# A depthwise convolution moved to TensorE, in 32-column tiles over four stacked shifts

## What is computed

```python
def _conformer_conv(h, w_pw1, b_pw1, w_dw, b_dw, ln_g, ln_b, w_pw2, b_pw2):
    u = h @ w_pw1 + b_pw1                                  # 1024 -> 2048
    u = u[..., :D_MODEL] * jax.nn.sigmoid(u[..., D_MODEL:])
    pad = (CONV_WIDTH - 1) // 2
    c = lax.conv_general_dilated(u, w_dw[:, None, :].astype(u.dtype),
        window_strides=(1,), padding=[(pad, pad)],
        dimension_numbers=("NWC", "WIO", "NWC"),
        feature_group_count=D_MODEL) + b_dw                # one filter of 31 taps per feature
    c = jax.nn.silu(_layernorm(c, ln_g, ln_b))
    return c @ w_pw2 + b_pw2
```

## Time and profile before

| | us |
|---|---|
| median of 3 runs | 1868.45 (1865.5 to 1893.15) |
| the profiled execution | 1865.6 |
| its span in the trace | 1863.8 |
| PE busy | 1720.8 (92%) |
| DVE busy | 1224.1 (66%) |
| ACT busy | 820.9 (44%) |
| GpSimd busy | 39.3 (2%) |
| mean granted TensorE clock | 0.966 of full speed |

### The profile page before, as it was taken

One profiled execution on the slowest core, in us unless ns is written; L12 is line 12 of the kernel. 1 busy time (PEld: TensorE's weight loads), 2 busy tenths in 40 slices (PEclk: granted clock), 3 DMA queues, 4 the chain that ended last, 5 costly groups with the idle time before them and its releaser, 6 DMA issues.

```text
span 1863.8 us, 29337 instructions
## 1 busy us (share of the span) xinstructions
PE 1720.8 (92%) x11365; PEld 1585.7 (85%) x11365; DVE 1224.1 (66%) x1756; ACT 820.9 (44%) x1229; POOL 39.3 (2%) x23
## 2 busy tenths in 40 slices
PE   7869999997888999999989879999999989689998
PEld 7857899996677999999988679998999989589997
DVE  4778575656767666766668867565666654866665
ACT  4556453335553434534352164334434344744433
POOL 0000000000013000000000000000000000000000
PEclk9979999998998999999999989999999999789999
DMA  7610245453234545445444035544445444035544
GB/s 269 213 46 1 91 181 191 180 188 116 102 103 149 188 180 192 169 176 195 173 145 134 1 125 203 193 179 176 174 170 201 169 148 168 1 104 213 190 179 159
DMA packets 53291, 285.93 MB, mean 153 GB/s; under 512 B 5872, under 2 KB 6128, under 8 KB 30704
## 3 DMA queue, kind: packets, MB, share of 16 engines
q1 hardware_dynamic: 52224, 281.46, 42.0%
q0 software_dynamic: 1008, 3.67, 0.6%
HBM read 284.05 MB, written 1.05 MB: 153 GB/s over the span
## 4 chain that ended last, share of the span: by engine, by line
PE 82%; DVE 11%; ACT 4%; issue 2%; DMA 0%; DVEq 0%; SPq 0%; ACTq 0%
PE bank L869 18%; PE bank L871 18%; PE bank L870 18%; PE bank L1052 9%; PE bank L1021 3%; PE bank L1023 3%; PE bank L1025 3%; DVE proj L1842 3%; PE bank L883 2%; PE bank L1109 1%; PE bank L1068 1%; PE bank L1089 1%; ACT whi L438 1%; DVE nmax L1559 1%; DVE att L1557 1%
## 5 line engine op out<-in xcount | busy, mean ns | idle before, releaser
L869 PE MATMUL bank<-hthi,whi 128*128 128x256 f32 x2144 | 607.9, 284 | 1.9 <-DVE wlo L1348 1.8
L870 PE MATMUL bank<-htlo,whi 128*128 128x256 f32 x2144 | 607.2, 283 | 0.0
L871 PE MATMUL bank<-hthi,wlo 128*128 128x256 f32 x2144 | 607.1, 283 | 0.0
L1342 DVE TENSOR_TENSOR wlo<-raw,whi 128x2048 fp32r<-128x2048 f32 x175 | 401.5, 2294 | 97.1 <-ACT whi L438 97.0
L869 PEld LDWEIGHTS bank<-hthi,whi 128*128 128x128 f32 x2144 | 411.6, 192 | 7.3 <-DVE wlo L1348 2.2
L870 PEld LDWEIGHTS bank<-htlo,whi 128*128 128x128 f32 x2144 | 411.6, 192 | 4.7
L871 PEld LDWEIGHTS bank<-hthi,wlo 128*128 128x128 f32 x2144 | 411.6, 192 | 0.0
L438 ACT ACTIVATE whi<-raw 128x2048 fp32r<-128x2048 f32 x175 | 334.2, 1910 | 35.5 <-PE bank L871 27.3
L521 ACT ACTIVATE tr<-tr 128x256 f32<-128x256 f32 x132 | 55.6, 421 | 656.7 <-DVE tr L1431 656.7
L1431 DVE TENSOR_TENSOR tr<-bank,rb 128x512 f32<-128x512 f32 x132 | 91.2, 691 | 231.0 <-PE bank L871 230.8
L1348 DVE TENSOR_TENSOR wlo<-raw,whi 128x1024 fp32r<-128x1024 f32 x174 | 214.6, 1233 | 23.2 <-ACT whi L446 23.0
(11 more groups left out here) (249 smaller groups left out, 2111.8 us busy)
## 6 DMA issues: line engine op xcount, KB each, us to landing
raw<-in_stream SPq DMA_DIRECT2D x176, 1024.0 KB, 5.2
raw<-in_stream SPq DMA_DIRECT2D x176, 512.0 KB, 3.5
wide<-in_wide POOLq DMA_DIRECT2D x7, 512.0 KB, 4.0
x<-in_x SPq DMA_DIRECT2D x1, 1024.0 KB, 5.5
out<-x SPq DMA_DIRECT2D x2, 512.0 KB, 2.9
wide<-in_const SPq DMA_DIRECT2D x1, 960.0 KB, 15.7
const<-in_const SPq DMA_DIRECT2D x1, 897.0 KB, 12.8
cols<-in_cols SPq DMA_DIRECT2D x1, 340.0 KB, 7.9
```

What stands on the lines that cost most here:

```text
L869: nc.tensor.matmul(out, whi_, mhi, start=start, stop=False)
L870: nc.tensor.matmul(out, whi_, mlo, start=False, stop=False)
L871: return nc.tensor.matmul(out, wlo_, mhi, start=False, stop=stop)
L1342: V.tensor_tensor(wlo[:, s, 0:UA], raw[:, s, 0:UA], whi[:, s, 0:UA].bitcast(F32), ALU.subtract)\
```

## The change

Every tap now runs on TensorE, and no diagonal is made on the chip.

- The 128 features of a chunk are four groups of 32. For each group a tile `stacked` holds four copies of its rows of `conv_u`, shifted by 0, 1, 2 and 3 tokens, on partitions 0 to 31, 32 to 63, 64 to 95 and 96 to 127. ACT starts one DMA for each copy, 16 per chunk, within SBUF (`stack`, 32 partitions x 284 elements, 36 KB each). Four chunks' tiles fit in what is free of `xn`, `att` and `proj`.
- One matmul then sums four taps of one group: 128 rows, weights 128 x 32, output on the 32 partitions of that group in the bank. Eight shifts by four groups are 32 matmuls per chunk (`convolve`), 256 in all, plain float32. `convolve(c)` is placed two chunks behind PW1; the last two stand behind it.
- The weights of the taps, 8 x 512 KB, come by DMA from a new input. GpSimd starts these eight in the second feed-forward block, one every second unit.
- ACT adds the bias of each chunk (`biased`), three chunks behind its own `stack`. The sums for the mean of chunks 0 to 4 stand ahead of `convolve(6)`, those of 5 to 7 behind `convolve(7)`. Subtraction and squaring are cut in four pieces where there were two.

```diff
+STACK = 4
+GROUP = P // STACK
+SHIFTS = -(-TAPS // STACK)
+UPITCH = 288
+SLOTS = 4
+BEHIND = 2
...
+        conv_bank = [acc[c % 4][:, (c // 4) * T:(c // 4 + 1) * T] for c in range(8)]
+        mean_bank, var_bank = tp[0][:, 0:T], tp[1][:, 0:T]
...
                 if n == 2:
-                    pool.wait_ge(s_ldi, 16)
-                    pool.wait_ge(s_ldc, 16)
                     pool.wait_ge(s_ol, 16)
                     pool.wait_ge(s_x, 12)
...
-                    for c, k, cnt, part, at in diag_runs:
-                        ins = nc.gpsimd.tensor_tensor(
-                            diag[part][:, at:at + cnt, :], ident.unsqueeze(1).to_broadcast([P, cnt, P]),
-                            dw[:, c, k:k + cnt].unsqueeze(2).to_broadcast([P, cnt, P]), ALU.mult)
...
+                    for c in range(8):
+
+                        pool.wait_ge(s_useb, U_F2 + 2 + 2 * c)
+                        pool.dma_start(tap_w[c].rearrange("p g q n -> p (g q n)"), taps_d[c]).then_inc(s_tap, 16)
...
+            def stack(c):
+
+                act.wait_ge(s_glu, c + 1)
+                if c >= SLOTS:
+                    act.wait_ge(s_dw, c - SLOTS + 1)
+                for g in range(STACK):
+                    for j in range(STACK):
+                        act.dma_start(stacked[c % SLOTS][g][j * GROUP:(j + 1) * GROUP, 0:UPITCH - STACK],
+                                      conv_u[g * GROUP:(g + 1) * GROUP, c, j:j + UPITCH - STACK])\
+                            .then_inc(s_stk[c % SLOTS], 16)
+
+            def biased(c):
+
+                act.wait_ge(s_dw, c + 1)
+                nc.scalar.activation(conv_c[:, c, :], conv_bank[c], ACT.Identity, bias=col("b_dw", c)).then_inc(s_cc, 1)
...
+                        stack(c)
+                        if c > BEHIND:
+                            biased(c - BEHIND - 1)
+            for c in range(7 - BEHIND, 8):
+                biased(c)
...
+            def convolve(c):
+
+                pe.wait_ge(s_tap, 16 * 8)
+                pe.wait_ge(s_stk[c % SLOTS], 16 * STACK * STACK * (c // SLOTS + 1))
+                if c >= 4:
+                    pe.wait_ge(s_cc, c - 3)
+                for q in range(SHIFTS):
+                    for g in range(STACK):
+                        ins = nc.tensor.matmul(conv_bank[c][g * GROUP:(g + 1) * GROUP, :], tap_w[c][:, g, q, :],
+                                               stacked[c % SLOTS][g][:, STACK * q:STACK * q + T],
+                                               start=q == 0, stop=q == SHIFTS - 1, skip_group_check=True)
+                ins.then_inc(s_dw, 1)
...
+                    if q % 2 and q // 2 >= BEHIND:
+                        convolve(q // 2 - BEHIND)
+            taken("r_conv", 1)
+            mean_of(range(0, 8 - BEHIND - 1))
+            for c in range(8 - BEHIND, 8):
+                convolve(c)
+            mean_of(range(8 - BEHIND - 1, 8)).then_inc(ev["mean_done"], 1)
```

More of the change, by code:

```diff
@@ L327, in build @@
         s_out = sem("stored")
+        s_tap = sem("tap_weights_loaded")
+        s_stk = [sem(f"stacked_{i}") for i in range(SLOTS)]
+        s_dw, s_cc = sem("chunk_convolved"), sem("chunk_biased")
         ev = {name: sem(name) for name in (
@@ L805, in _ @@
                                              bias=col("b_pw1", 8 + c)).then_inc(s_sig, 1)
[L806 to L811 removed]
+                        stack(c)
[3 more added lines that the diff above has]
+                biased(c)
+            for q in range(4):
                 act.wait_ge(ev["centred"], q + 1)
[L813 removed]
+                h = slice(2 * q, 2 * q + 2)
                 nc.scalar.activation(conv_s[:, h, :], conv_c[:, h, :], ACT.Square).then_inc(ev["sq_ready"], 1)
             act.wait_ge(ev["var_done"], 1)
[L816 removed]
+            nc.scalar.activation(conv_r[:, 0, :], var_bank, ACT.Sqrt, bias=LN_EPS)\
                 .then_inc(ev["conv_std"], 1)
@@ L1243, in _, with mean_of @@
             ffn(2, 4)
+            def convolve(c):
[9 more added lines that the diff above has]
+                ins.then_inc(s_dw, 1)
+            def mean_of(chunks_):
+                for c in chunks_:
+                    pe.wait_ge(s_cc, c + 1)
+                    ins = nc.tensor.matmul(mean_bank, ones, conv_c[:, c, :], start=c == 0, stop=c == 7)
+                return ins
             ready = x_operand("op_conv", 5)
@@ L1833, in _ @@
             V.memset(conv_u[:, :, PAD + T:], 0.0)
-            def conv_taps(chunks_, k0, k1, ready=None):
-                for k in range(k0, k1):
-                    for c in chunks_:
-                        w = col("w_dw", k * 8 + c)
-                        if k == 0:
-                            ins = V.tensor_scalar(conv_c[:, c, :], conv_u[:, c, 0:T], w, col("b_dw", c), ALU.mult, ALU.add)
-                        else:
-                            ins = V.scalar_tensor_tensor(out=conv_c[:, c, :], in0=conv_u[:, c, k:k + T], scalar=w,
-                                                         in1=conv_c[:, c, :], op0=ALU.mult, op1=ALU.add)
-                    if k < k1 - 1 or ready is None:
-                        own(ins)
-                if ready is not None:
-                    ins.then_inc(ready, 1)
             for w, chunks in enumerate(PW1):
@@ L1866, in _ @@
                                                in1=sg[:, c % 2, :], op0=ALU.add, op1=ALU.mult).then_inc(s_glu, 1)
-            dve.wait_ge(s_glu, 8)
-            conv_taps((0, 1), 5 * EARLY, TAPS, ready=ev["conv_early"])
-            conv_taps(range(2, CONV_DVE), 0, SPLIT)
-            conv_taps(range(2, SHARED), SPLIT, TAPS)
-            dve.wait_ge(ev["conv_summed"], 2)
-            V.tensor_tensor(conv_c[:, SHARED, :], conv_c[:, SHARED, :], acc[1][:, 0:T], ALU.add).then_inc(ev["conv_ready"], 1)
             dve.wait_ge(ev["mean_done"], 1)
-            mean = acc[0][:, 0:T].unsqueeze(1).to_broadcast([P, 4, T])
-            for q in range(2):
-                h = slice(4 * q, 4 * q + 4)
+            mean = mean_bank.unsqueeze(1).to_broadcast([P, 2, T])
+            for q in range(4):
+                h = slice(2 * q, 2 * q + 2)
                 V.tensor_tensor(conv_c[:, h, :], conv_c[:, h, :], mean, ALU.subtract).then_inc(ev["centred"], 1)
@@ L1879, in _ @@
             own(V.reciprocal(conv_r[:, 1, :], conv_r[:, 0, :]))
-            dve.wait_ge(ev["centred"], 2)
+            dve.wait_ge(ev["centred"], 4)
             for q in range(5):
@@ L2017, in lay_wide, with lay_taps @@
     return np.stack([post[0, 0], a["conv_b_pw2_2"][0], mix[0], post[0, 1], post[1, 0], mix[1], post[1, 1]])
+def lay_taps(a):
+    w = np.zeros((SHIFTS * STACK, 8, STACK, GROUP), np.float32)
+    w[0:TAPS] = a["conv_w_dw_2"].reshape(TAPS, 8, STACK, GROUP)
+    out = np.zeros((8, STACK, GROUP, STACK, SHIFTS, GROUP), np.float32)
+    n = np.arange(GROUP)
+    out[:, :, n, :, :, n] = w.reshape(SHIFTS, STACK, 8, STACK, GROUP).transpose(4, 2, 1, 3, 0)
+    return out.reshape(8, P, STACK * SHIFTS * GROUP)
 def shape_constants():
```

82 lines of the change are left out of this document (15 added, 67 removed).

## The result

| | before | changed |
|---|---|---|
| median of 4 runs, us | 1868.64 (1865.5 to 1893.15) | 1910.4 (1898.94 to 1923.83) |
| the profiled execution, us | 1865.6 | 1899.51 |
| its span, us | 1863.8 | 1897.7 |

The ratio is 1.0215, 95% interval 1.0142 to 1.0287: slower, by 1.4 to 2.9%. So compared the changed kernel is 31 us (1.7%) slower: 1899.4 against 1868.2 us and 1924.8 against 1893.8 us, medians of all runs of this study.

What follows compares the result with a forecast made beforehand. DVE's taps bounded the 57.1 us from PW1's end to the mean; ACT's copy issues would replace them. 1865.6 + 19.0 (ACT-paced stretch) + 2.0 (clock) - 11.5 (diagonals) - 1.2 (behind mean) = 1873.9, forecast 1874 us; range 1850 to 1919 us.

Steps and rivals of the forecast that it cites:

- both slower rivals: Convolution tiles running serially (1915.7 us, chance 0.21) and ACT issues dearer than SP's (1916 us, chance 0.11).
- rival 1: PE's convolution: four column tiles side by side, 3.4 us per chunk, issues priced the same, 1867 us; chance 0.25.
- rival 3: ACT's copy issues in PW1 dearer than SP's, 0.73 us plus a 0.05 us gap: +42 us, 1916 us; chance 0.11.
- I take 0.45 us, near the straight-line code that ACT's is too.: Price of each ACT copy issue in PW1: 7.2 us a chunk, 57.6 us for eight.
- The relay: PW1, between six units: hi copies, remainder, scaling, sigmoid and product before the next issues, 6.85 us five times, 34.3 us.
- I take two: PE's convolution: two column tiles work at once, so a chunk costs 6.9 us.
- Rival 2: PE's convolution: tiles run one after the other, 13.8 us a chunk, PE the bound, 1915.7 us; chance 0.21.
- The clock, +2.0 us: Last convolutions and means: PE at its lower clock after idling, +2.0 us, between 0 and 2.5.
- the tail: After chunk 7's last issue: an eviction, means and two convolutions up to the mean's end, 17.8 us, plus 2.0 for clock.
- The landing hidden, the tap weights free: Copy landings hidden behind two chunks, or means and a convolution; 4 MB of tap-weight loads at 0, +3 us in the range.
- -11.5 us for the diagonals: Second feed-forward block: GpSimd no longer makes diagonals while DVE's instructions stretch, -11.5 us, bound 0.
- -1.2 us behind the mean: Subtraction and squaring in half-size pieces let PE's sums over the squares start earlier: -1.2 us, between -2 and 0.

Runs made afterwards that it cites:

- Experiment 1: Changed kernel with each chunk's 16 copies issued by SyncE (SP) instead of ACT: 1861.2 us in the shorter group, median 1883.5 us in the longer.
- experiment 4: Changed kernel with each of ACT's 16 copies a chunk cut from 32 rows to 8: 1898.97 us.
- experiment 6: Changed kernel with the convolution's two loops exchanged, so one column tile's eight shifts follow each other before the next tile's: 1934.0 us (longer group).
- experiment 8: Kernel before, its 109 diagonals loaded by 13 GpSimd DMAs instead of multiplied out: 1858.3 to 1860.7 us (shorter group), 1881 to 1884, once 1889 (longer).
- experiment 3: Changed kernel with only the unshifted copy of each group of 32 channels, 4 of a chunk's 16 copies, all passes kept: 1853.4 us (longer group).

## Why the prediction was right and where it was not

The forecast was 1874 us and "no change"; the time lies in the range, on its slow side. The mechanism held in outline: the 57 us of DVE's taps went, ACT's issues took their place, and PE idled in front of each unit. But the sum is 26 us under the profiled execution, and the range, 69 us wide because it took in both slower rivals, covers that. Two of the prediction's own signs of being wrong came true: passes 0.054 us apart (rival 1) and issues above 0.6 us (rival 3). It was luck that they pull in opposite directions, -7.5 against +27.8 us. What the steps gave:

- **"I take 0.45 us, near the straight-line code that ACT's is too."** This is the step that went wrong. 16 issues took 10.2 to 11.2 us, 85.4 us in place of 57.6: +27.8 us, more than the whole error. The rows behind it were SP's issues of other transfers. Experiment 1 shows that the engine was not the difference, since SP pays 0.59 us for these copies too, and experiment 4 that the rows of a copy are not it either. What makes the loads of the stream cheaper to issue stays open. Rival 3 was right in kind and too dear in size (0.78 us a copy).
- **The relay.** 6.85 us were read from one passage; the first in the changed kernel is 6.87 us (965.83 to 972.70), right. The last two take 9.0 us (1044.11 to 1053.14), so the gaps between stacks sum to 42.9 us and not 38.2: +4.7 us. I had taken one passage for all five. In the last two VectorE also waits for PE, 2.08 us each, 4.2 of the 4.7 us; in the passage that I read nothing waits for PE. PE works there at a granted clock of 0.50.
- **"I take two"** (column tiles at once). Wrong: four, 3.66 us a chunk, as rival 1 had it. It mattered little, 12.3 us of tail in place of 17.8 + 2.0, since ACT was the bound. The second pass of a tile does wait for its first, 0.216 us in experiment 6, but that does not hold up the tiles behind it: passes of another tile start ahead of up to three that stand before them in the program. The rule that matmuls start in program order, from which I had 6.9 us, does not hold across tiles here. Rival 2 falls, and experiment 6 shows what serial tiles cost.
- **The clock, +2.0 us.** `convolve(6)` and `convolve(7)` took 8.94 us, against 2 x 3.66 = 7.3: 1.6 us. Right for the tail, but the clock was down after the waits in PW1 too, and in the last two relays that showed, which I had not priced.
- **The landing hidden, the tap weights free.** Right: 1.4 us of wait in all for the copies; and the loop's first matmuls of the third block moved from 778.58 to 766.93 us, by 11.65 us, as those of the second, so the 4 MB cost nothing between.
- **-11.5 us for the diagonals.** Right: 11.5 us in the stretch itself (18.96 against 30.44), and experiment 8 shows the cause alone. At the start of the marked-off stretch 11.3 us of it are left.
- **-1.2 us behind the mean.** 1.0 us at the first sum over the squares (1.4 against 2.4 us), 0.7 us at the end.

Put together: 19.0 + 2.0 + 27.8 + 4.7 - 7.5 (the tail, 17.8 + 2.0 - 12.3) = 46.0 us for the stretch, and it is 45.9.

Tiles that take turns need 3.66 us for 64 passes, one after another 11.43 us. The Trainium skill (TensorEngine Tiling (Array Packing), Tiling Modes) has different tiles loading and multiplying in parallel; the trace agrees. The cost of the small copies is in their issues, 0.61 us each, and not in the landing, 1.9 us and hidden. Of the Trainium skill's advice to join small transfers (DMA: Bandwidth & Descriptors, Rules for kernel authors) the runs show only this side, that fewer are better (experiment 3); no run joins them.

## What to carry to other kernels

A DMA start is an instruction of the engine that it stands on, here 0.5 to 0.65 us for each small copy, and no less when it carried a quarter; count it as work of that engine, and put many of them on one that the path does not need (GpSimd here, with the convolution one chunk later: 40 us better than before, where ACT made it 31 us worse). Ask first what stands behind them in that engine's order, since the order alone was half of what ACT's issues cost the stretch. An issue's price must come from an issue of the same kind; where only another kind is in the trace, let the range and the chances carry the doubt.

## What the runs showed of the hardware

- **One issue, three engines.** The same 32 x 284 copy within SBUF: 0.61 us on ACT, 0.59 on SP, 0.50 on GpSimd; with 8 rows 0.63 us on ACT. Of SP's loads from memory some took less, 0.34 and 0.45 us.
- **Column tiles in plain float32.** Four tiles of 32 columns start their passes together, four passes in 0.215 us. Passes of the same tile in a row start 0.216 us apart, and where one tile's row of passes ends, the next tile's first four run beside its last four (experiment 6).
- **One stage, either clock.** From 495 to 545 us, in an attention stage that the change does not touch, TensorE's granted clock is 0.97 to 1.00 in the traces of the shorter group and 0.50 to 0.53 in those of the longer; first before, then the changed kernel again:

```profile
495.00:545.00 50.00, 46.03 (x237) 34.55 (x236) 30.64 (x66) 24.52 (x55) 0.00 (x0) 0.99 0.19 63
```

```profile
495.00:545.00 50.00, 45.14 (x111) 24.55 (x110) 23.52 (x53) 13.18 (x47) 0.00 (x0) 0.53 0.06 21
```

PE is about as busy in both (46.0 and 45.1 of 50 us), with half the matmuls. What decides the clock here, the runs do not show.
